# Third branch summed on VectorE, high-part products first, low parts awaited by halves, in a fused transformer kernel on one Trainium2 core

## The chip, the cores and the metric

One core of one Trainium2 chip runs the whole program. The metric is the device time of one execution in microseconds (us). The engines are called here as in the profile: PE is TensorE (matmuls), with its weight loads as PEld; DVE is VectorE, ACT is ScalarE, POOL is GpSimd, and SP only issues DMAs.

## The reference

Twelve sublayers are applied to a [256, 1024] tensor of float32: two blocks of two layers, each layer a feed-forward net, a mixing sublayer and a second feed-forward net, each between norms and with a residual. Cut to what the change touches:

```python
def swiglu_ffn(h, w_gu, w_down):
    a, b = jnp.split(h @ w_gu, 2, axis=-1)
    return (jax.nn.silu(a) * b) @ w_down

def mixing_sublayer(h, w_in, ...):            # block 1
    z = h @ w_in
    ...                                        # four branches of width 256
    gates = jax.nn.sigmoid(gz.reshape(B, S, N_BRANCH, D_MODEL))
    y = gates[:, :, 0] * (branches[0] @ w_branch[0])
    for n in range(1, N_BRANCH):
        y = y + gates[:, :, n] * (branches[n] @ w_branch[n])
    return y @ w_out
```

Block 2 is alike, with three branches and with shifts beside the norm gains.

## The kernel before

**Stages.** A stage is one sublayer; its key is block, layer, kind: `10f1`, `10m`, `10f2`, `11f1`, `11m`, `11f2`, then `20f1` to `21f2`. In the profiled execution `10m` begins at about 211 us, `10f2` at 413, `11f1` at 607, `11m` at 799, `11f2` at 1004, `20f1` at 1198, `20m` at 1392, `20f2` at 1618, `21f1` at 1808, `21m` at 1998 and `21f2` at 2223 us.

**Split numbers.** Each float32 operand is split in a high part (float32r) and a low part, the rest. A product of two operands is three matmuls that add up in PSUM: high by high, high by low, low by high (`three`). For activations the parts are `NH` and `NL`, for weights `hi` and `lo`. ACT makes `hi` from `raw` (`split_hi`), DVE makes `lo` as `raw` minus `hi` (`split_lo`, or in two halves by `split_lo_half`).

**Units.** Every stage reads 33 weight units of 128x2048 (two DMAs each, on SP's queue). A unit's `raw` and `lo` share one of five slots, `hi` has one of four. PE waits for `lo_ready` of a unit (`ready(s, u)`) before its first matmul, and releases the unit with `unit_used`.

**Where a stage begins.** The 256 tokens are two tiles t of 128. While the last matmuls of a stage run for tile 1, tile 0 is normed on DVE, transposed on PE (`turn_normed`), copied to `NH` by ACT (`normed`) and its rest put into `NL` by DVE (`normed_rest`), each in two halves of four 128-column chunks. `nh t a` and `nl t a` are the signals of tile t, half a. PE then multiplies tile 0 with units 0 to 3. Meanwhile DVE does for tile 1, in its fixed order (`entrance`): the products with the gain row (L1175), the low part of unit 2, the new X (L1193), the low part of unit 3, the mean square (L1204) that POOL turns into an inverse root, the norm (L1234; in block 2 also a shift, L1240). For stages of block 2 the new X comes before both units. PE turns tile 1 before the last quarter of unit 3 (in a mixing stage too), and then multiplies tile 1 with units 0 to 3.

**Where a mixing stage ends.** Units 25 to 28 hold the four branch projections, 29 to 32 the output projection. In block 1 PE does branches 2 and 3 together: the first half of the columns of branch 2, of branch 3, then the second halves. DVE multiplies each result, in pieces b of 128x512, with its gates (`gated`, L1688). POOL adds branches 0 and 1 (`sum 1 b`, L680) and then branch 2 (`sum 2 b`, L680 too); DVE adds branch 3 (`merged`, `y b`, L1697), ACT copies the high part (`yh b`, L1083), DVE makes the low part (`yl b`, L1700). PE starts the output projection, unit 29, when `yl 0` is there; its order is unit 29 and 30 for tile 0, 29 for tile 1, then 31 and 32 for tile 0 and the rest of tile 1.

The order on every engine is that of the code; only semaphores tie the engines. In the block-1 mixing stage the code before reads:

```python
if u == OUT1 - 1:                    # u = 28
    if s.block == 1:
        gated(G[:, 16:24, :], 2, range(0, 2))
        merged(G[:, 24:32, :], 3, "sum 2", range(0, 2))
        gated(G[:, 16:24, :], 2, range(2, 4))
```

## Time and profile before

| what | value |
|---|---|
| three timed runs | 2421.65, 2423.36, 2424.78 us, median 2423.36 |
| the profiled execution's own time | 2421.88 us |
| its span in the profile | 2420.1 us |
| mean granted TensorE clock | 0.999 |
| PE busy | 2388.7 us, 99% of the span |
| PEld busy | 2178.4 us, 90% |
| DVE busy | 1651.3 us, 68% |
| ACT busy | 1208.5 us, 50% |
| POOL busy | 233.8 us, 10% |

The span is the time from the first to the last recorded instruction. Busy times of different engines overlap. Matmuls are pipelined: a 128x512 matmul is shown with 0.39 us, but the next one starts 0.23 us after it (a 128x256 one: 0.12 us after it), so PE's rate is read from starts.

### The profile page before, as it was taken

The page shows a single profiled execution, that of the slowest core. Times are in us where ns is not written, and L with a number is a line of the kernel's source. Part 1 is how long each engine was busy: PE and PEld are TensorE (multiplying, and loading weights), DVE is VectorE, ACT ScalarE, POOL GpSimd, SP SyncE. Part 2 cuts the span into 40 slices and gives each one's busy share as a digit, 9 for nine tenths or more (in the row PEclk, how much of TensorE's full clock was granted, in tenths as well). Part 3 has the DMA queues.
Part 4 walks back from the last instruction along what each step waited for, and adds up shares of the span by engine and source line. Part 5 has one row for each costly group of instructions (what it writes and reads, how often), then busy time and mean ns, then how long its engine had stood idle before and what let it go on. Part 6 is the DMA issues. An engine that isn't in the chain of part 4 may idle for free. (4 is left out here: it accounts for less than half of the span.)

```text
span 2420.1 us, 39354 instructions
## 1 busy us (share of the span) xinstructions
PE 2388.7 (99%) x16673; PEld 2178.4 (90%) x16673; DVE 1651.3 (68%) x2158; ACT 1208.5 (50%) x1448; POOL 233.8 (10%) x334
## 2 busy tenths in 40 slices
PE   8999999999999999999999999999999999999998
PEld 6998998898899999799889899889988989988997
DVE  4786877787786697788678665575555556557554
ACT  5445565434434556444443456944444445694443
POOL 2000003000200000300110001210001000121000
PEclk9999999999999999999999999999999999999999
DMA  8895556797887564689589665456656655545653
GB/s 280 296 309 168 175 164 220 258 305 234 290 299 242 161 183 158 229 290 304 180 302 306 206 170 150 131 184 209 201 183 205 189 176 170 153 130 190 212 183 114
DMA packets 371551, 514.59 MB, mean 213 GB/s; under 512 B 23712, under 2 KB 312726, under 8 KB 371376
## 3 DMA queue, kind: packets, MB, share of 16 engines
q1 hardware_dynamic: 344976, 415.80, 53.5%
q0 software_dynamic: 26400, 96.28, 11.7%
q8 instruction: 132, 2.16, 0.4%
q14 instruction: 43, 0.35, 0.0%
HBM read 510.89 MB, written 1.13 MB: 212 GB/s over the span
## 5 line engine op out<-in xcount | busy, mean ns | idle before, releaser
L1141 DVE TENSOR_TENSOR lo<-raw,hi 128x2048 fp32r<-128x2048 f32 x382 | 876.7, 2297 | 436.4 <-ACT hi L743 435.4
L743 ACT ACTIVATE hi<-raw 128x2048 fp32r<-128x2048 f32 (+2 forms) x393 | 749.3, 1910 | 475.7 <-PE ps L1780 206.2
L1780 PE MATMUL ps<-NH,hi 128*128 128x256 f32 x3360 | 951.2, 283 | 0.0
L1780 PE MATMUL ps<-NL,hi 128*128 128x256 f32 x3360 | 942.1, 280 | 0.0
L1780 PE MATMUL ps<-NH,lo 128*128 128x256 f32 x3360 | 940.5, 280 | 0.0
L1780 PEld LDWEIGHTS ps<-NH,hi 128*128 128x128 f32 x3360 | 632.4, 188 | 13.5 <-issue 10.1
L1780 PEld LDWEIGHTS ps<-NL,hi 128*128 128x128 f32 x3360 | 633.2, 188 | 3.1
L1780 PEld LDWEIGHTS ps<-NH,lo 128*128 128x128 f32 x3360 | 634.1, 189 | 0.0
L1780 PE MATMUL ps<-hi,NH 128*128 128x512 f32 (+4 forms) x768 | 280.5, 365 | 12.4 <-DVE lo L1141 6.6
L1780 PE MATMUL ps<-hi,BH 128*128 128x512 f32 (+1 forms) x768 | 291.6, 383 | 0.0
L1780 PE MATMUL ps<-hi,BL 128*128 128x512 f32 (+1 forms) x768 | 288.6, 379 | 0.0
L1780 PE MATMUL ps<-lo,BH 128*128 128x512 f32 (+1 forms) x768 | 288.4, 379 | 0.0
L1780 PE MATMUL ps<-lo,NH 128*128 128x512 f32 (+4 forms) x768 | 274.2, 357 | 0.0
L1780 PE MATMUL ps<-hi,NL 128*128 128x512 f32 (+4 forms) x768 | 274.1, 357 | 0.0
L1294 DVE SCALAR_TENSOR_TENSOR T<-arena,T 128x512 f32<-128x512 f32 x252 | 188.5, 748 | 3.8
L1780 PEld LDWEIGHTS ps<-hi,NH 128*128 128x128 f32 x768 | 145.1, 189 | 43.4 <-DVE lo L1141 12.1
L1780 PEld LDWEIGHTS ps<-hi,BL 128*128 128x128 f32 (+1 forms) x768 | 139.3, 181 | 30.7
L805 ACT ACTIVATE BH<-arena 128x256 fp32r<-128x256 f32 x128 | 53.6, 419 | 224.8 <-DVE arena L1268 224.8
L1780 PEld LDWEIGHTS ps<-hi,NL 128*128 128x128 f32 x768 | 145.2, 189 | 22.7
L1780 PEld LDWEIGHTS ps<-lo,NH 128*128 128x128 f32 x768 | 145.4, 189 | 19.9
L1780 PEld LDWEIGHTS ps<-hi,BH 128*128 128x128 f32 (+1 forms) x768 | 139.2, 181 | 26.7 <-DVE BL L1280 0.5
L1780 PEld LDWEIGHTS ps<-lo,BH 128*128 128x128 f32 (+1 forms) x768 | 139.4, 182 | 26.3
(316 smaller groups left out, 1997.2 us busy)
## 6 DMA issues: line engine op xcount, KB each, us to landing
raw<-in_ffn_w_in SPq DMA_DIRECT2D x176, 512.0 KB, 4.9
raw<-in_ffn_w_gu SPq DMA_DIRECT2D x174, 512.0 KB, 5.7
arena<-in_ada_w POOLq DMA_DIRECT2D x72, 1024.0 KB, 6.3
raw<-in_w_in SPq DMA_DIRECT2D x92, 512.0 KB, 4.6
raw<-in_ffn_w_down SPq DMA_DIRECT2D x88, 512.0 KB, 4.4
raw<-in_ffn_w_out SPq DMA_DIRECT2D x88, 512.0 KB, 4.4
raw<-in_mix_w_in SPq DMA_DIRECT2D x86, 512.0 KB, 4.6
raw<-in_w_branch SPq DMA_DIRECT2D x16, 512.0 KB, 4.1
```

What stands on the lines that cost most here:

```text
L743: last = nc.scalar.activation(dst, src, ACT.Copy)
L805: nc.scalar.activation(BH[:, 2 * (g % 2) + j, :], HF[:, j, :], ACT.Copy).then_inc(act_done, done("act", f"bh {g} {j}"))
L1141: last = nc.vector.tensor_tensor(dst, src, part.bitcast(F32), ALU.subtract)
L1294: ins = nc.vector.scalar_tensor_tensor(out=ada_acc, in0=ADW[:, c, :], scalar=cond[:, c:c + 1], in1=ada_acc, op0=ALU.mult, op1=ALU.add)
L1780: last = nc.tensor.matmul(dst, a, b, start=start and k == 0, stop=stop and k == 2, skip_group_check=skip)
```

## The change

1. **End of the mixing stage, block 1.** POOL no longer adds branch 2. A new `third` adds it on DVE, one 128x512 addition per piece. `last_two` writes out DVE's order: products of branch 2, pieces 0 and 1, their sums, branch 3 and `y` of pieces 0 and 1, a product of branch 2, the low parts of y (`low_y`), and only then the low part of unit 30, which stood ahead of all that; then the second half of the columns. In block 2 the same work stays in the same order.
2. **High part first.** At the start of each stage, for the first chunks of unit 0 (and of unit 1 in some stages) and for both tiles, PE issues all products with `NH` first, after `nh`, and those with `NL` after them, after `nl`. The number of matmuls is the same.
3. **Halves.** The low part of unit 3 is made in two halves, as unit 1's was, and PE waits for unit 1 and unit 3 by halves (`lo half 1`, `lo half 3`). In text the title's "second and fourth unit" are units 1 and 3.
4. **Setup.** ACT copies the first half of `NH` before it waits for the second half of unit 0.

```diff
-                    if s.block == 1 and u in (BR1 + 1, BR1 + 2):
+                    if s.block == 1 and u == BR1 + 1:
...
             act.wait_ge(first_in, 32)
             nc.scalar.activation(hi[:, 0, 0:1024], raw[:, 0, 0:1024], ACT.Copy).then_inc(act_done, done("act", "hi first"))
+            normed(None, 0, range(1))
             act.wait_ge(raw_ready[0], 32)
             nc.scalar.activation(hi[:, 0, 1024:2048], raw[:, 0, 1024:2048], ACT.Copy).then_inc(hi_ready, 1)
-            normed(None, 0)
+            normed(None, 0, range(1, 2))
...
-                split_lo(s, 3)
+                for k in range(2):
+                    split_lo_half(s, 3, k)
                 mean_square_new(p, 1)
...
+            def third(pairs):
 
                 for b in pairs:
-                    gated(gates, n, (b,))
-                    mine(f"gated {n}" if b == 3 else f"gated {n} {b}")
-                    dve.wait_ge(pool_done, at("pool", f"{sum_before} {b}"))
+                    mine("gated 2" if b == 3 else f"gated 2 {b}")
+                    dve.wait_ge(pool_done, at("pool", f"sum 1 {b}"))
                     y = T8[:, 2 * b:2 * b + 2, :]
-                    nc.vector.tensor_tensor(y, y, gates[:, 2 * b:2 * b + 2, :], ALU.add).then_inc(dve_done, done("dve", f"y {b}"))
+                    nc.vector.tensor_tensor(y, y, G[:, 16 + 2 * b:18 + 2 * b, :], ALU.add).then_inc(dve_done, done("dve", f"sum 2 {b}"))
...
+            def last_two(s):
+
+                fourth = G[:, 24:32, :]
+                gated(G[:, 16:24, :], 2, range(0, 2))
+                third(range(0, 2))
+                merged(fourth, 3, None, range(0, 2))
+                gated(G[:, 16:24, :], 2, range(2, 3))
+                low_y(range(0, 2))
+                split_lo(s, OUT1 + 1)
+                gated(G[:, 16:24, :], 2, range(3, 4))
+                third(range(2, 4))
+                merged(fourth, 3, None, range(2, 4))
+                low_y(range(2, 4))
...
                 else:
                     ready(s, 0)
+                    pe.wait_ge(act_done, at("act", "nh 0 0", p))
+                    gate_up(0, 0, 0, 0, parts=range(0, 2))
                     pe.wait_ge(dve_done, at("dve", "nl 0 0", p))
-                    gate_up(0, 0, 0, 0)
-                ready(s, 1)
...
                 ready(s, 2)
                 gate_up(2, 0, 1, 0)
+                pe.wait_ge(dve_done, at("dve", "lo half 3", p))
+                gate_up(3, 1, 1, 0, range(0, 2))
                 ready(s, 3)
-                gate_up(3, 1, 1, 0, range(0, 3))
+                gate_up(3, 1, 1, 0, range(2, 3))
                 turn_normed(p, 1)
...
                 bank_free(0, 1)
+                pe.wait_ge(act_done, at("act", "nh 1 0", p))
+                gate_up(0, 0, 0, 1, parts=range(0, 2))
                 pe.wait_ge(dve_done, at("dve", "nl 1 0", p))
-                gate_up(0, 0, 0, 1).then_inc(unit_used, 1)
+                gate_up(0, 0, 0, 1, parts=range(2, 3)).then_inc(unit_used, 1)
```

**How the instructions move.** On DVE at the end of the first mixing stage (`10m`), before. `arena<-arena,ps` is a product with gates, `T8<-T8,arena` an addition, `NL<-T8,NH` a low part of y, and the first `lo<-raw,hi` is unit 30, the last three are units 31, 32 and the next stage's 0:

```order
L1141 TENSOR_TENSOR lo<-raw,hi 128x2048 [waits hi_ready]
L1688 TENSOR_TENSOR arena<-arena,ps 128x512 [waits pe_done] x3
L1697 TENSOR_TENSOR T8<-T8,arena 128x512 [waits pool_done,dve_done]
L1688 TENSOR_TENSOR arena<-arena,ps 128x512 [waits pe_done]
L1697 TENSOR_TENSOR T8<-T8,arena 128x512 [waits pool_done,dve_done]
L1700 TENSOR_TENSOR NL<-T8,NH 128x512 [waits act_done] x2
L1688 TENSOR_TENSOR arena<-arena,ps 128x512 [waits pe_done] x3
L1697 TENSOR_TENSOR T8<-T8,arena 128x512 [waits pool_done,dve_done]
L1688 TENSOR_TENSOR arena<-arena,ps 128x512 [waits pe_done]
L1697 TENSOR_TENSOR T8<-T8,arena 128x512 [waits pool_done,dve_done]
L1700 TENSOR_TENSOR NL<-T8,NH 128x512 [waits act_done] x2
L1141 TENSOR_TENSOR lo<-raw,hi 128x2048 [waits hi_ready] x3
```

And the same place after, up to the third and fourth of the additions at L1699 (the first row holds the four products of branch 1 too, which another `lo` no longer parts from those of branch 2):

```order
L1691 TENSOR_TENSOR arena<-arena,ps 128x512 [waits pe_done] x6
L1699 TENSOR_TENSOR T8<-T8,arena 128x512 [waits pool_done,dve_done] x2
L1691 TENSOR_TENSOR arena<-arena,ps 128x512 [waits pe_done]
L1732 TENSOR_TENSOR T8<-T8,arena 128x512 [waits dve_done]
L1691 TENSOR_TENSOR arena<-arena,ps 128x512 [waits pe_done]
L1732 TENSOR_TENSOR T8<-T8,arena 128x512 [waits dve_done]
L1691 TENSOR_TENSOR arena<-arena,ps 128x512 [waits pe_done]
L1705 TENSOR_TENSOR NL<-T8,NH 128x512 [waits act_done] x2
L1139 TENSOR_TENSOR lo<-raw,hi 128x2048 [waits hi_ready]
L1691 TENSOR_TENSOR arena<-arena,ps 128x512 [waits pe_done]
L1699 TENSOR_TENSOR T8<-T8,arena 128x512 [waits pool_done,dve_done] x2
```

Four additions are new on DVE (L1699), and unit 30's low part has moved behind the first two low parts of y.

On PE in stage `10f2`, from the transposes of the hidden tile (first row) to tile 1 with unit 0, before:

```order
L1840 MATMUL ps<-arena 128x128
L1780 MATMUL ps<-hi,NH 128x512 [waits dve_done]
L1780 MATMUL ps<-lo,NH 128x512
L1780 MATMUL ps<-hi,NL 128x512
L1780 MATMUL ps<-hi,NH 128x512
```

And after:

```order
L1870 MATMUL ps<-arena 128x128
L1810 MATMUL ps<-hi,NH 128x512 [waits act_done,dve_done]
L1810 MATMUL ps<-lo,NH 128x512
L1810 MATMUL ps<-hi,NH 128x512
L1810 MATMUL ps<-lo,NH 128x512
L1810 MATMUL ps<-hi,NH 128x512
L1810 MATMUL ps<-lo,NH 128x512
L1810 MATMUL ps<-hi,NH 128x512
L1810 MATMUL ps<-lo,NH 128x512
L1810 MATMUL ps<-hi,NL 128x512 [waits dve_done]
L1810 MATMUL ps<-hi,NL 128x512 x3
```

The wait for `nl 1 0` stands eight matmuls later; the `dve_done` that is left at the first one is that of the PSUM bank.

On DVE at the entry to `11f1` and its like, before and after: the low part of unit 3 between the new X and the mean square.

```order
L1193 SCALAR_TENSOR_TENSOR X<-arena,X 128x1024 [waits dve_done,pool_done]
L1141 TENSOR_TENSOR lo<-raw,hi 128x2048 [waits hi_ready]
L1204 TENSOR_SCALAR arena<-arena 128x1 [waits act_done]
L1234 SCALAR_TENSOR_TENSOR arena<-X,arena,T 128x512 [waits pre_in,pool_done]
L1234 SCALAR_TENSOR_TENSOR arena<-X,arena,T 128x512
```

```order
L1194 SCALAR_TENSOR_TENSOR X<-arena,X 128x1024 [waits dve_done,pool_done]
L1150 TENSOR_TENSOR lo<-raw,hi 128x1024 [waits hi_ready] x2
L1205 TENSOR_SCALAR arena<-arena 128x1 [waits act_done]
L1235 SCALAR_TENSOR_TENSOR arena<-X,arena,T 128x512 [waits pre_in,pool_done]
L1235 SCALAR_TENSOR_TENSOR arena<-X,arena,T 128x512
```

One instruction has become two; nothing else moved there.

## Rows read from the trace of the kernel before

**Rows 1.** The page, busy time, share of the span, instructions:

```profile
PE 2388.7 (99%) x16673; PEld 2178.4 (90%) x16673; DVE 1651.3 (68%) x2158; ACT 1208.5 (50%) x1448; POOL 233.8 (10%) x334
```

**Rows 2.** PE's waits: total us, times, longest:

```profile
PE ps L1780 <- DVE lo L1141: 6.6, 14, 0.8
PE ps L1780 <- DVE NL L1250: 2.9, 7, 1.0
```

**Rows 3.** Timeline, entry to `11f1`: start, duration, [idle before <-releaser]:

```profile
614.22 2.28 DVE L1141 TENSOR_TENSOR lo<-raw,hi 128x2048 fp32r<-128x2048 f32 x1
615.66 0.39 PE L1780 MATMUL ps<-hi,NL 128*128 128x512 f32 x1
616.56 0.50 PE L1780 MATMUL ps<-hi,NH 128*128 128x512 f32 x1 [0.51 <-DVE lo L1141]
617.23 1.42 DVE L1234 SCALAR_TENSOR_TENSOR arena<-X,arena,T 128x512 f32<-128x512 f32 x2 [0.66 <-POOL arena L510]
618.75 1.03 PE L1807 MATMUL ps<-arena 128*128 128x128 f32 x8
619.39 1.09 ACT L792 ACTIVATE NH<-ps 128x512 fp32r<-128x512 f32 x2 [3.89 <-PE ps L1807]
619.54 0.48 PE L1780 MATMUL ps<-hi,NH 128*128 128x512 f32 x1
620.33 0.38 PE L1840 MATMUL ps<-arena 128*128 128x128 f32 x2
620.86 0.47 PE L1780 MATMUL ps<-hi,NH 128*128 128x512 f32 x1
```

**Rows 4.** Timeline of DVE, a half split and the next instruction:

```profile
1196.86 1.22 DVE L1149 TENSOR_TENSOR lo<-raw,hi 128x1024 fp32r<-128x1024 f32 x1
1197.99 1.28 DVE L1250 SCALAR_TENSOR_TENSOR NL<-ps,NH 128x512 fp32r<-128x512 f32 x2
```

**Rows 5.** Timeline of PE, tile 1 turned at the entry to `20f1`:

```profile
1210.65 1.26 PE L1807 MATMUL ps<-arena 128*128 128x128 f32 x8 [0.39 <-DVE arena L1240]
1211.66 0.48 PE L1780 MATMUL ps<-hi,NH 128*128 128x512 f32 x1
...
1212.45 0.38 PE L1840 MATMUL ps<-arena 128*128 128x128 f32 x2
1212.81 0.47 PE L1780 MATMUL ps<-hi,NH 128*128 128x512 f32 x1
```

**Rows 6.** Timeline of PE, first matmul of tile 1 in `10m` and `20m`:

```profile
224.87 0.39 PE L1780 MATMUL ps<-hi,NH 128*128 128x256 f32 x1 [0.26 <-DVE NL L1250]
...
1405.85 0.39 PE L1780 MATMUL ps<-hi,NH 128*128 128x256 f32 x1 [0.35 <-DVE NL L1250]
```

**Rows 7.** Timeline, end of `10m`:

```profile
377.86 7.11 POOL L680 TENSOR_TENSOR T<-arena 128x512 f32<-128x512 f32 x4 [29.16 <-DVE arena L1688]
380.50 3.30 DVE L1141 TENSOR_TENSOR lo<-raw,hi 128x2048 fp32r<-128x2048 f32 x1 [0.93 <-ACT hi L743]
385.90 2.54 POOL L680 TENSOR_TENSOR T<-T,arena 128x512 f32<-128x512 f32 x2
391.08 0.47 PE L1780 MATMUL ps<-hi,NH 128*128 128x512 f32 x1 [0.64 <-DVE NL L1700]
395.41 0.68 DVE L1688 TENSOR_TENSOR arena<-arena,ps 128x512 f32<-128x512 f32 x1
396.12 0.69 DVE L1697 TENSOR_TENSOR T<-T,arena 128x512 f32<-128x512 f32 x1
396.73 1.47 DVE L1700 TENSOR_TENSOR NL<-T,NH 128x512 fp32r<-128x512 f32 x2
398.12 6.69 DVE L1141 TENSOR_TENSOR lo<-raw,hi 128x2048 fp32r<-128x2048 f32 x3
400.46 0.50 PE L1780 MATMUL ps<-hi,NH 128*128 128x512 f32 x1 [0.81 <-DVE lo L1141]
```

**Rows 8.** Timeline of PE, end of `11m`, units 29 and 31:

```profile
980.30 0.47 PE L1780 MATMUL ps<-hi,NH 128*128 128x512 f32 x1 [1.79 <-DVE NL L1700]
...
989.69 0.50 PE L1780 MATMUL ps<-hi,NH 128*128 128x512 f32 x1 [0.78 <-DVE lo L1141]
```

**Rows 9.** Timeline of PE, setup, units 0 and 2:

```profile
14.49 0.77 PE L1780 MATMUL ps<-hi,NH 128*128 128x512 f32 x1 [0.54 <-DVE NL L1250]
...
23.17 0.50 PE L1780 MATMUL ps<-hi,NH 128*128 128x512 f32 x1 [0.23 <-DVE lo L1141]
```

More of the change, by code:

```diff
@@ L1147, in split_lo_half @@
                 dve.wait_ge(hi_ready, n + 1)
-                part = slice(1024, 8 * VU_N if (s.kind, s.block, u) == ("m", 1, V_U) else 2048) if k else slice(0, 1024)
-                last = nc.vector.tensor_tensor(lo[:, n % LR, part], raw[:, n % LR, part], hi[:, n % HR, part].bitcast(F32), ALU.subtract)
+                (dst, src), = split_pieces(s, u, n % LR, lo)
+                (part, _), = split_pieces(s, u, n % HR, hi)
+                half = dst.shape[1] // 2
+                cols = slice(half * k, half * k + half)
+                last = nc.vector.tensor_tensor(dst[:, cols], src[:, cols], part[:, cols].bitcast(F32), ALU.subtract)
                 if k:
@@ L1152, in split_lo_half @@
                 else:
-                    last.then_inc(dve_done, done("dve", "lo half"))
+                    last.then_inc(dve_done, done("dve", f"lo half {u}"))
             def tile_out(s, t, h):
@@ L1325, in ffn @@
                     mean_square_new(p, 1)
-                    split_lo(s, 3)
+                    for k in range(2):
+                        split_lo_half(s, 3, k)
                 else:
@@ L1734, in mix @@
                         gated(G2[:, 8:16, :], 2)
-                    if u == OUT1 - 1:
-                        if s.block == 1:
-                            merged(G[:, 24:32, :], 3, "sum 2", range(2, 4))
-                        else:
-                            merged(G2[:, 16:24, :], 1, "sum 1", range(2, 4))
+                    if u == OUT1 - 1 and s.block == 2:
+                        merged(G2[:, 16:24, :], 1, "sum 1", range(2, 4))
+                        low_y(range(2, 4))
                 split_lo(s, OUT1 + 2)
@@ L1774, in ready, with three @@
                 pe.wait_ge(lo_ready, s.base + u + 1)
-            def three(dst, wh, wl, xh, xl, start, stop, weights_still=True, skip=False):
+            def three(dst, wh, wl, xh, xl, start, stop, weights_still=True, skip=False, parts=range(3)):
                 pairs = ((wh, xh), (wh, xl), (wl, xh)) if weights_still else ((xh, wh), (xh, wl), (xl, wh))
                 for k, (a, b) in enumerate(pairs):
+                    if k not in parts:
+                        continue
                     last = nc.tensor.matmul(dst, a, b, start=start and k == 0, stop=stop and k == 2, skip_group_check=skip)
@@ L1793, in channels, with tokens @@
                 return last
[L1795 removed]
+            def tokens(dst, u, n, a, w, t, chunks=range(C), parts=range(3)):
                 for c in chunks:
                     wh, wl = weights(u, n * c + a, n * c + a + w)
[L1799 removed]
+                    last = three(dst, NH[:, c, tile_of(t)], NL[:, c, tile_of(t)], wh, wl, c == 0, c == C - 1, True, skip=True, parts=parts)
                 return last
@@ L1810, in turn_normed, with gate_up @@
                     m.stage = stage
-            def gate_up(u, half, g, t, chunks=range(4)):
+            def gate_up(u, half, g, t, chunks=range(4), parts=range(3)):
                 for c in chunks:
@@ L1816, in gate_up @@
                     k = 4 * half + c
-                    last = three(ps[:, gu_bank(g, t), :], NH[:, k, tile_of(t)], NL[:, k, tile_of(t)], wh, wl, k == 0, k == C - 1, True, skip=True)
+                    last = three(ps[:, gu_bank(g, t), :], NH[:, k, tile_of(t)], NL[:, k, tile_of(t)], wh, wl, k == 0, k == C - 1, True, skip=True, parts=parts)
                 return last
```

85 lines of the change are left out of this document (55 added, 30 removed).

## The prediction

> **What bounds the kernel now.** I began with the page: PE is busy for 2388.7 of 2420.1 us [rows 1]. So the change, which takes no matmul away, can give back only time in which PE stands still, about 31 us, of which the first 10 lie before any matmul. Then came PE's waits: for low parts of weights 6.6 us in 14 waits, for low parts of activations 2.9 us in 7 [rows 2]. Where these waits lie was read from the timeline of PE: at each of the eleven stage boundaries, at the end of the two block-1 mixing stages, and in the setup; inside stages PE runs from one matmul to the next.
>
> The idle time that the view shows is less than what is lost. At the entry to 11f1 the last matmul of unit 2 starts at 615.66 and the first of unit 3 at 616.56, 0.90 us later where 0.23 is usual: 0.67 lost, 0.51 shown [rows 3]. So I add 0.16 to each idle time shown. A pair of transposes normally holds PE for 0.15 us (my estimate from their 0.38 us, which overlaps); in 11f1 the matmul after them comes 0.53 later, which is 0.38 lost without a releaser named [rows 3]: it is the wait for the low part of tile 1.
>
> What matters at every place is which wait comes next, since DVE's work for tile 1 is a chain of its own that starts from the end of the previous stage.
>
> **The change, part by part.** All is costed as PE time regained.
>
> *Entry to a block-1 feed-forward stage (10f2, 11f1, 11f2).* In 11f1 the low part of unit 3 runs from 614.22 to 616.50, and PE, ready at 615.89, starts at 616.56 [rows 3]. A half takes 1.22 us [rows 4], so the first is there at 615.44 and the second at about 616.56, when PE does not ask for it before 615.89 + 6 x 0.23 = 617.27. The 0.67 us go. What is late next is the norm of tile 1: its two halves start at 617.23 and take 1.42, the first is done at about 617.94. PE would be at the transposes at 618.75 - 0.67 = 618.08, so just behind the first half and ahead of the second. How long the transposes take then, rows of another stage show: there PE waits for both halves, and from the first transpose to the next matmul it is 1.01 us [rows 5], here now 0.79 [rows 3]. So 618.08 + 1.01 = 619.09 and some 0.05 for the later norm, against 619.54: 0.4 regained of 0.67. Then the high part first: ACT copies the first half of NH between 619.39 and about 619.94, in time, and with its wait eight matmuls later the low part is no longer waited for: 0.38. Together 0.78, three times: **2.3 us**. In 11f2 PE also waits early in the stage for tile 0's low part (the longest wait of that kind, 1.0 [rows 2]); that wait goes too, but DVE's chain there is set by weights that come late, so PE meets the chain again at unit 3; I count nothing for it.
>
> *What a half costs.* A half and the next instruction start 1.13 us apart [rows 4], full splits (6.69 - 2.28) / 2 = 2.20 apart [rows 7]: two halves cost 0.06 us more, on the chain to the norm. The Trainium skill ("VectorE: DVE Perf Modes", the section on the TRN2 errata) speaks against such a cut: it says that an operation with sources in SBUF pays a fixed extra latency per instruction, and gives (N + 151) / 0.96 ns for a float32 tensor_tensor, that is 0.16 us for each further instruction, an estimate from that page. By it the gain would be 0.7 us smaller over the seven feed-forward entries. The starts in the rows say 0.06, and these decide here.
>
> *Entry to a block-1 mixing stage (10m, 11m).* Matmuls are 256 wide there, and PE comes to the norm with more room. The stall at unit 3 (about 0.45) returns nearly whole, and the first matmul of tile 1 waits 0.26 + 0.16 [rows 6] for its low part, which ends. 0.85 twice: **1.7 us**.
>
> *Entry to a block-2 mixing stage (20m, 21m).* DVE makes the new X before both units there, so PE's stall lies at unit 2, which is not cut. Only the low part of tile 1: 0.35 + 0.16 [rows 6], and the first matmul after a stall is slower by 0.1: 0.6 twice: **1.2 us**.
>
> *Entry to a block-2 feed-forward stage (20f1, 20f2, 21f1, 21f2).* Here the norm is what PE waits for already: the transposes begin with an idle 0.39 and take 1.01 instead of 0.79 [rows 5]. The stall at unit 3 of 20f1 moves there and gains nothing; the halves cost 0.06. After the transposes of the hidden tile it is 0.36 to the next matmul [rows 5] against 0.15: 0.21 regained. 0.15 four times: **0.6 us**.
>
> *Setup.* PE starts 0.54 us earlier if it may begin on NH [rows 9], but unit 2, whose weights are still coming, holds it to 23.17 as before [rows 9]; what is left are a short wait at unit 3 and 0.38 at tile 1: **0.5 us**.
>
> *End of a block-1 mixing stage.* In 10m PE loses 0.64 + 0.16 before unit 29 and 0.81 + 0.16 before unit 31 [rows 7], together 1.8; in 11m 1.79 + 0.16 and 0.78 + 0.16 [rows 8], together 2.9. POOL's four sums of branches 0 and 1 take 7.11 us [rows 7]; two later ones take 2.54, 1.27 each [rows 7], so 5.08 of the 7.11 are their own. The low part of unit 30 falls into them and takes 3.30 instead of 2.28 [rows 7]: one waits for the other to end. With that split moved away POOL is done at 377.86 + 5.08 = 382.94. DVE has the products of branch 2 (pieces 0, 1) at about 382.2, so its first addition waits to 382.94. From there its order is a chain: two additions 1.22; for pieces 0 and 1 a product and an addition, 0.71 + 0.61 from the starts at 395.41, 396.12 and 396.73 [rows 7], 2.64; a product 0.62; two low parts 1.39 (396.73 to 398.12 [rows 7]); the low part of unit 30, 2.20; then 0.62 + 1.22 + 2.64 + 1.39. The sum is 13.9: unit 31's low part starts at 396.9 instead of 398.12 [rows 7]. The low part for unit 29 is there at about 388, before PE wants it at 390.3; unit 30's at 391, before 393.1. So the first stall goes whole and the second stays, and 398.12 - 396.87 = 1.25 is regained in 10m. In 11m DVE is earlier by its place against POOL's sums: its first addition comes while POOL's third sum runs, and POOL's fourth gets in behind it and holds the second addition for 1.27. So 1.3 there, or 2.5 if it does not get in. Together **2.55 us**, with bounds of 0 (each addition waits again) and 4.7 (both stalls of both stages).
>
> The transfers of the next stage start from two signals: unit 29 used, and the last low part of y. Both come earlier by about as much as PE, so I count nothing.
>
> **The sum.** 2.3 + 1.7 + 1.2 + 0.6 + 0.5 + 2.55 = 8.85 us. Against the profiled execution's own 2421.88 that is 2413.0; the median of the runs is 1.48 above it, and I forecast for the median: 2423.36 - 8.85 = **2414.5 us**. A measurement tells some 0.2%, 4.85 us, from no change.
>
> **Rivals.**
> 1. *The ends of the mixing stages gain nothing*: the four additions, 2.44 us more on DVE, eat what the shorter chain gives, and unit 31 is as late as before. For it: DVE is the last releaser at both stalls. Against: the waits for POOL go. Time: 8.85 - 2.55 = 6.3 gained, 2417.1. Chance 0.16.
> 2. *DVE becomes the bound and the kernel is slower.* If all four new additions had to wait for a sum of POOL, 4 x 1.27 = 5.1 us, unit 31 would come 5.1 - 1.25 = 3.9 later than now, twice 7.7, and with the norms late in the next stages most of the rest goes: about 2430. It decides once the four wait for over 1.25 together. Against: POOL has no sum left after 383, and DVE's third and fourth come at about 391. Chance 0.04.
> 3. *The stalls only move.* At each entry PE meets the norm of tile 1 instead, as in block 2 now [rows 5]: the halves give nothing, tile 1's part is hidden by later norms, and 2 to 4 us in all remain: 2420.5. For it: DVE's chain from the previous stage is fixed. Against: in 11f1 the norm is done in time for all but 0.25 us. Chance 0.12.
> 4. *All stalls go*: DVE is through with its order before PE in both mixing stages and 11f2 regains its early wait: 12 to 13 us, 2411. Chance 0.06.
>
> My own case has 0.62. The range reaches from rival 4 to the middle of rival 3: 2409.5 to 2420.5; forecast, rival 1 and rival 4 lie inside, with part of rival 3. Faster by over 4.85 us: 0.62 + 0.13 of rival 1 + 0.06, 0.81. Within: the rest of rivals 1 and 3, 0.15. Slower 0.04.
>
> **What the changed profile would show.** Right: no idle before unit 3 in block 1; no idle named after NL before tile 1 anywhere; 0.2 to 0.3 us more between the transposes and the next matmul in 11f1; unit 29 started without a wait at the end of 10m and 11m, and unit 31 still waiting for a low part, by 0.4 to 1.8; POOL's four sums in about 5.1 us instead of 7.11. Wrong: an addition of DVE after 385 that lasts over 1 us; a wait for unit 30; a new wait for NH; or ACT late with the next stage's unit 1. The forecast fails if the 0.16 that I add to each idle time, or the 0.38 at tile 1, is not PE's loss but something that stays.

## The result, and the profile after

The changed kernel takes 2412.37 us (median of 5 runs, 2410.64 to 2413.22) against 2421.96 (2421.20 to 2424.78) for the kernel before on the same chip: a ratio of 0.9957, 95% interval 0.9946 to 0.9968, or 9.6 us. The forecast was 8.85 us less, 2414.5. The profiled execution took 2412.04 us, with a span of 2410.2 us at a granted clock of 0.999.

The page's row of busy times:

```profile
PE 2385.2 (99%) x16673; PEld 2177.2 (90%) x16673; DVE 1651.8 (69%) x2178; ACT 1208.4 (50%) x1448; POOL 220.5 (9%) x326
```

and the view of PE's waits (engine, line, releaser: us in total, times, longest):

```profile
PE ps L1837 <- DVE arena L1235: 9.9, 2, 9.6
PE ps L1810 <- DVE lo L1139: 4.3, 8, 0.8
PE ps L1837 <- DVE arena L1241: 1.7, 2, 1.3
PE ps L1810 <- DVE arena L1270: 0.8, 1, 0.8
PE ps L2208 <- DVE arena L1574: 0.4, 1, 0.4
```

Beside [rows 2]: no matmul waits for NL any more, the waits for low parts of weights fell from 6.6 us in 14 to 4.3 in 8, and one of 0.8 us is new (a bias addition, L1270, in 10f1; below). The wait of 1.3 us (L1241) stands before the transposes of tile 1 in 20f1, where it was 0.39 [rows 5]: the stall of 0.53 before unit 3 there has moved to the norm, as forecast. PE is busy for 2385.2 us, 3.5 less than before; the rest of the gain is idle time.

**An entry.** PE's timeline at the entry to 11f1 (start, duration in us, engine, line, operation), which answers to [rows 3]:

```profile
615.26 0.40 PE L1810 MATMUL ps<-hi,NL 128*128 128x512 f32 x1
615.62 1.32 PE L1837 MATMUL ps<-arena 128*128 128x128 f32 x8
616.70 0.48 PE L1810 MATMUL ps<-hi,NH 128*128 128x512 f32 x1
```

There is no stall before unit 3. The transposes begin 0.13 late and hold PE for 1.08 us to the next matmul, where it was 0.79: the norm of tile 1 is what comes next, as forecast.

**An end.** The end of 10m on GpSimd, VectorE and TensorE (first the sums of branches 0 and 1; L1691 are products, L1699 the new additions, L1705 low parts of y, L1139 splits). It answers to [rows 7]:

```profile
377.50 5.06 POOL L677 TENSOR_TENSOR T<-arena 128x512 f32<-128x512 f32 x4 [29.16 <-DVE arena L1691]
...
379.85 0.69 DVE L1691 TENSOR_TENSOR arena<-arena,ps 128x512 f32<-128x512 f32 x1 [0.64 <-PE ps L1810]
381.26 0.69 DVE L1691 TENSOR_TENSOR arena<-arena,ps 128x512 f32<-128x512 f32 x1 [0.72 <-PE ps L1810]
381.87 1.84 DVE L1699 TENSOR_TENSOR T<-T,arena 128x512 f32<-128x512 f32 x2
...
388.08 2.28 DVE L1139 TENSOR_TENSOR lo<-raw,hi 128x2048 fp32r<-128x2048 f32 x1
...
394.73 1.47 DVE L1705 TENSOR_TENSOR NL<-T,NH 128x512 fp32r<-128x512 f32 x2
396.13 4.49 DVE L1139 TENSOR_TENSOR lo<-raw,hi 128x2048 fp32r<-128x2048 f32 x2
```

GpSimd's four sums take 5.06 us instead of 7.11. The low part of unit 31 starts 18.63 us after the first of them (396.13 - 377.50), where it was 398.12 - 377.86 = 20.26 [rows 7]. PE shows no wait for unit 29 and none for unit 31, so both stalls of 10m are gone.

**Where the time came from.** A span from the first transpose of one kind to the next is a clock that all these kernels share: "entry" runs from the transposes of tile 0 at the end of the stage before to those of tile 1, "rest" from there to those of tile 0 at the stage's own end. Worked out from the starts of these rows in the PE timelines, in us:

| | before | changed | changed again | ends only | entries only | no high first | order only | sum only | unit 3 whole |
|---|---|---|---|---|---|---|---|---|---|
| 10f1 rest | 181.04 | 181.77 | 180.69 | 181.86 | 180.81 | 181.06 | 180.65 | 180.69 | 180.67 |
| 10m entry | 13.53 | 12.94 | 12.95 | 13.52 | 12.91 | 12.95 | 12.94 | 12.95 | 13.51 |
| 10m rest | 190.21 | 188.17 | 188.18 | 188.76 | 190.03 | 188.76 | 190.41 | 188.12 | 188.01 |
| 10f2 entry | 13.46 | 12.91 | 12.81 | 13.45 | 13.76 | 13.76 | 12.81 | 14.30 | 14.19 |
| 11f1 entry | 13.46 | 12.80 | 12.81 | 13.45 | 12.82 | 12.80 | 12.81 | 12.82 | 13.45 |
| 11m rest | 191.11 | 188.08 | 188.89 | 189.61 | 190.83 | 188.24 | 190.71 | 187.91 | 187.74 |
| 11f2 entry | 14.62 | 14.12 | 14.41 | 14.68 | 14.71 | 14.48 | 12.81 | 14.24 | 15.00 |
| 20m rest | 213.35 | 212.81 | 212.77 | 213.35 | 212.74 | 213.28 | 212.87 | 212.90 | 212.60 |
| 20f2 entry | 13.35 | 13.42 | 13.42 | 13.35 | 13.42 | 13.41 | 13.42 | 13.43 | 13.37 |

Some rows repeat over all kernels with the same code there (10m entry and 11f1 entry to 0.04 us, 20m rest to 0.16), others differ by about 1 us and more with the same code (10f1 rest, 10f2 entry, 11m rest). That difference matters for every reading below.

A narrower window shows the ends by themselves. The same matmul is taken in the trace of before and in another trace, and the difference of its two starts is read once ahead of unit 29 and once behind the first products of unit 31 (389.13 and 403.82 us in the 10m of before, 977.42 and 990.03 in its 11m). What the difference grows by in between is what PE gained over that end, in us. The last row is how long ScalarE waited for a late transfer of w_out in 11m (3.82 in before):

| | changed | changed again | ends only | entries only | no high first | order only | sum only | unit 3 whole |
|---|---|---|---|---|---|---|---|---|
| end of 10m | 1.65 | 1.66 | 1.65 | 0.00 | 1.64 | -0.40 | 1.72 | 1.68 |
| end of 11m | 2.59 | 1.85 | 1.58 | -0.10 | 2.81 | 0.02 | 2.84 | 2.80 |
| wait for w_out, 11m | 2.90 | 3.79 | 4.06 | 3.91 | none | 3.39 | 2.68 | 2.53 |

### The profile page after: what moved, and what is told of

It is laid out like the page before. It is cut to its first block and busy times, and to the rows that moved or that the text cites. A ratio compares the mean times of both kernels' runs of the same rounds, so it can differ in the third digit from the quotient of the medians.

```text
span 2410.2 us, 39367 instructions
## 1 busy us (share of the span) xinstructions
PE 2385.2 (99%) x16673; PEld 2177.2 (90%) x16673; DVE 1651.8 (69%) x2178; ACT 1208.4 (50%) x1448; POOL 220.5 (9%) x326
## 3 DMA queue, kind: packets, MB, share of 16 engines
HBM read 510.89 MB, written 1.13 MB: 212 GB/s over the span
## 5 line engine op out<-in xcount | busy, mean ns | idle before, releaser
L1139 DVE TENSOR_TENSOR lo<-raw,hi 128x2048 fp32r<-128x2048 f32 (+1 forms) x370 | 848.4, 2294 | 435.3 <-ACT hi L740 434.1
L1810 PE MATMUL ps<-hi,NL 128*128 128x512 f32 (+4 forms) x768 | 259.3, 357 | 0.0
```

Of the source, the lines that this page charges most:

```text
L1139: last = nc.vector.tensor_tensor(dst, src, part.bitcast(F32), ALU.subtract)
L1810: last = nc.tensor.matmul(dst, a, b, start=start and k == 0, stop=stop and k == 2, skip_group_check=skip)
```

## Experiments

All times are medians beside runs of the kernel before on the same chip. There were several chips, so kernels from different ones are compared by their distance from before, which took 2422.68 us beside the first four kernels, 2422.30 beside the changed kernel run again and the three named with it, 2422.12 beside the three with transposes apart, and 2421.51 beside the kernel with the early split. The intervals of the ratios are 4 to 6.5 us wide, so a difference of 1 or 2 us between two kernels rests on the traces and not on the medians.

### The ends alone, and the entries alone

Two halves of the change. The first is the kernel before with `last_two`, `third` and GpSimd's shorter sums; the second the changed kernel with these put back:

```
                         if s.block == 1:
-                            last_two(s)
+                            gated(G[:, 16:24, :], 2, range(0, 2))
+                            merged(G[:, 24:32, :], 3, "sum 2", range(0, 2))
+                            gated(G[:, 16:24, :], 2, range(2, 4))
```

> The kernel before with only the ends of the block-1 mixing stages changed (third branch's sum on VectorE, the low part of unit 30 behind it, PE's wait for it); entries, setup and the order of products as before. Theory A (the parts are independent): the traces of before and after show PE 1.65 us earlier over the end of 10m and 2.6 over that of 11m, so 4.25 us faster than before, about 2417.7 us; POOL's first four sums take about 5.1 us, unit 29 starts without a wait, and the stalls at unit 3 and at tile 1 stay as they were. Rival B (the ends gain nothing by themselves, and what the shift showed there came from the earlier entries, which gave VectorE a lead): under 1.5 us, about 2421. Rival C (the forecast's size): 2.55 us, 2419.4.

> The changed kernel with the ends of the block-1 mixing stages put back as before (GpSimd sums branch 2, the low part of unit 30 early); setup, entries and order of products as changed. Theory A (independent parts): the pieces of the shift outside the two ends sum to about 5.4 us, so 2416.6 us, and together with the ends-only kernel the whole gain of 9.6. Rival B (the entries' gain is used up by the unchanged ends: PE arrives earlier and waits longer for units 29 and 31, since VectorE's chain there does not move): the entries of 10m and 11m give nothing, 1.7 to 2 us less, 2418.5. In the trace A has the stalls before units 29 and 31 of the length of [rows 7] and [rows 8], B has them longer by what the entry gave.

Ends only: 2419.53 us against 2422.68 (ratio 0.9988, 0.9979 to 0.9997), 3.15 less. Entries only: 2415.91 (0.9972, 0.9961 to 0.9983), 6.8 less. Together 9.9, the whole. In the kernel with entries only, the stalls of 10m and 11m are of the length of [rows 7] and [rows 8]:

```profile
389.69 0.47 PE L1788 MATMUL ps<-hi,NH 128*128 128x512 f32 x1 [0.64 <-DVE NL L1706]
399.08 0.50 PE L1788 MATMUL ps<-hi,NH 128*128 128x512 f32 x1 [0.81 <-DVE lo L1142]
...
977.79 0.47 PE L1788 MATMUL ps<-hi,NH 128*128 128x512 f32 x1 [1.89 <-DVE NL L1706]
987.18 0.50 PE L1788 MATMUL ps<-hi,NH 128*128 128x512 f32 x1 [0.78 <-DVE lo L1142]
```

So the parts add up (theory A of both), and rival B of both falls. The size in theory A of the first, 4.25, was read from one pair of traces and is too high: in the ends-only kernel the ends are worth 1.65 in 10m and 1.58 in 11m, 3.2, which is what its median shows, where 2.55 was forecast. (Its 10m rest is shorter by 1.45 only, because PE loses 0.2 more there between 248 and 258 us, far from the end; the entries-only kernel has the same loss.)

### High part first, and the halves of unit 3

```
-                pe.wait_ge(act_done, at("act", "nh 1 0", p))
-                gate_up(0, 0, 0, 1, parts=range(0, 2))
                 pe.wait_ge(dve_done, at("dve", "nl 1 0", p))
-                gate_up(0, 0, 0, 1, parts=range(2, 3)).then_inc(unit_used, 1)
+                gate_up(0, 0, 0, 1).then_inc(unit_used, 1)
```

and so at tile 0 and in the mixing stages:

> The changed kernel with the products of the first chunks in their old order (low parts of the activations waited for before the first product), in every entry but the setup; the halves of units 1 and 3 and the ends stay. Theory A (high part first is worth the idle at tile 1, and halves the rest): 0.38 in three block-1 feed-forward entries, 0.42 in two mixing entries, 0.6 in two of block 2 and 0.21 in four, together 4.0 us over the changed kernel, 2416.4. Rival B (the halves alone let the norm come early enough, so the low part of tile 1 is there in time too): within 1 us of the changed kernel, 2412.4 to 2413.4.

2417.66 us (0.9979, 0.9970 to 0.9988), 5.0 under before, where the changed kernel is 9.6 to 9.7 under: 4.6 over the changed kernel. Theory A said 4.0, and the 0.6 between them is within the noise; rival B falls. The waits for NL are back, in the view of waits and in two rows of PE's timeline, one of 10f2's tile 0 and one of 20m's tile 1:

```profile
PE ps L1810 <- DVE NL L1251: 3.1, 5, 1.5
```

```profile
414.44 0.47 PE L1810 MATMUL ps<-hi,NH 128*128 128x512 f32 x1 [0.76 <-DVE NL L1251]
1403.36 0.39 PE L1810 MATMUL ps<-hi,NH 128*128 128x256 f32 x1 [0.35 <-DVE NL L1251]
```

In the mixing stages it costs 0.4 in 10m (its rest is 0.59 longer, of which 0.2 is the loss between 248 and 258 us named above) and 0.47 to 0.51 in 20m. In 10f2 and 11f2 PE now also waits 0.76 and 1.5 for the low part of tile 0, which the sum left out; but these entries, 13.76 and 14.48 us, are no longer than in some kernels with the high part first (up to 14.30 and 14.71), so that these waits cost time is not shown. The runs of this kernel lie between 2414.45 and 2419.51, and the profiled one also waits 1.9 for a bias addition in 11f1.

The halves of unit 3 undone, and in the mixing stages PE's wait for unit 1 by halves too; the rest kept:

```
-                for k in range(2):
-                    split_lo_half(s, 3, k)
+                split_lo(s, 3)
...
-                pe.wait_ge(dve_done, at("dve", "lo half 3", p))
-                gate_up(3, 1, 1, 0, range(0, 2))
                 ready(s, 3)
-                gate_up(3, 1, 1, 0, range(2, 3))
+                gate_up(3, 1, 1, 0, range(0, 3))
```

> The changed kernel with unit 3's low part whole again and waited for whole (and in the mixing stages unit 1 waited for whole too); high part first and the ends stay. Theory A (my sum): 0.4 more in three block-1 feed-forward entries and 0.43 in two mixing ones, less 0.06 for each half saved in 9 places: 2.1 - 0.5 = 1.5 us over the changed kernel, 2413.9. Rival B (the stall only moves to the norm of tile 1, so that the halves give nothing): within 0.4 us, 2412.4 to 2412.8. Rival C (the whole stall of 0.67 comes back in each of five): 3.3 us over, 2415.7. In the trace A has a wait for a low part at unit 3 in block 1 and transposes of 11f1 without a wait.

2414.99 us (0.9967, 0.9955 to 0.9979). Its profiled execution took 7173.94 us where its other five took 2413.55 to 2416.62, and nothing is read from it; the kernel was run once more.

> The same kernel as the one without halves of unit 3, whose profiled execution was of no use (7174 us). Theory A as there: 0.4 us more in each of three block-1 feed-forward entries and two mixing entries, 0.06 less in nine; read from the stretches between the transposes of tile 0 and tile 1: 10f2 and 11f1 13.2 to 13.3 (changed 12.91 and 12.80, before 13.46 twice), 10m and 11m 13.4 (changed 12.95, before 13.52), block 2 as before within 0.1. Rival B (only moved to the norm): the stretches up to the transposes as before, but the next ones shorter by as much, with no difference to the changed kernel over both.

2414.91 us (0.9969, 0.9958 to 0.9981): 2.3 over the changed kernel run beside it, and by the distance from before 1.9 the first time; theory A said 1.5, rival C 3.3. The stall is back before unit 3, here in 11f1, and the entries of 10m and 11f1 are as long as before (13.51 and 13.45):

```profile
614.61 0.50 PE L1808 MATMUL ps<-hi,NH 128*128 128x512 f32 x1 [0.51 <-DVE lo L1139]
```

In 11f1 and 10m the halves are worth 0.65 and 0.56 at the entry, and the rest of the stage gives back about 0.15 in 10m. The rival by which the stall only moves falls for block 1. It holds for block 2: there the entry to 20f2 is 13.42 with halves and 13.37 without, so the halves gain nothing and cost 0.05 to 0.07 us a pair, the 0.06 of the forecast. By the Trainium skill ("VectorE: DVE Perf Modes", the section on the TRN2 errata) it would be about 0.16, an estimate from its formula; the stages here show a third of it.

### What of the ends does it: the order, or the sum

Once with the third branch summed on GpSimd again (cut to two lines here) and the low part of unit 30 in its new place; once with the sum on VectorE and unit 30's low part in its old place:

```
-                third(range(0, 2))
-                merged(fourth, 3, None, range(0, 2))
+                merged(fourth, 3, "sum 2", range(0, 2))
```

```
                 low_y(range(0, 2))
-                split_lo(s, OUT1 + 1)
...
-                        if u < OUT1 - (2 if s.block == 1 else 1):
+                        if u < OUT1 - 1:
                             split_lo(s, u + 3)
```

> The changed kernel with the third branch summed on GpSimd again, as before; the low part of unit 30 stays behind the first half of the y pieces, and all else stays. Theory A (the gain of the ends comes from taking unit 30's split out of GpSimd's four sums): GpSimd's sums take 5.1 us, its sums of branch 2 end 2.5 later and hold VectorE's first y pieces, VectorE has 2.4 us less work of its own; unit 31's low part starts 18.8 us after GpSimd's first sum in 10m (changed 18.6, before 20.3): within 0.5 us of the changed kernel over both stages. Rival B (the gain comes from not waiting for GpSimd's sum of branch 2): unit 31's low part starts at 20 us or later, and 1.5 to 3 us of time come back.

> The changed kernel with the low part of unit 30 in its old place, ahead of the products of branch 2; the third branch stays summed on VectorE, and all else stays. Theory A (the order carries the gain): GpSimd's four sums take 7.1 us again and the split 3.1 to 3.3; unit 29 waits 0.5 us in 10m and 0.9 in 11m, unit 31's low part starts 18.9 us after GpSimd's first sum; 0.5 to 1.5 us slower than the changed kernel. Rival B (the sum on VectorE carries it): within 0.3 us of the changed kernel. Rival C (additions of VectorE now lie against GpSimd's late sums as well, and each pair costs another 1.27): over 2.5 us slower.

Order only: 2415.05 us (0.9970, 0.9958 to 0.9981), 2.4 over the changed kernel run beside it. Over the end of 10m it loses 0.40 us against before, over that of 11m it is even (0.02). 11f2's entry, which follows the longer stall, takes 12.81 instead of 14.41 and gives part of it back; that the one comes of the other is likely but not shown. Sum only: 2413.58 us (0.9964, 0.9951 to 0.9976), with 1.72 and 2.84 gained over the two ends, as much as in the changed kernel. Its median is 1.0 over the changed kernel's, inside what theory A said (0.5 to 1.5) and outside rival B's 0.3, so the time does not decide between them. The traces do: in the profiled execution what is lost lies elsewhere, in 10f2's entry (14.30) and in 11f1 (180.53 for its rest against 178.51), with weights that landed late in both, and PE waits for neither unit 29 nor unit 31, where theory A had waits of 0.5 and 0.9. Theory A, my own, falls in both, and the mechanism of rival B holds in both. The order-only kernel in 10m:

```profile
376.64 5.05 POOL L680 TENSOR_TENSOR T<-arena 128x512 f32<-128x512 f32 x4 [29.16 <-DVE arena L1694]
382.62 2.54 POOL L680 TENSOR_TENSOR T<-T,arena 128x512 f32<-128x512 f32 x2
387.73 1.67 POOL L680 TENSOR_TENSOR T<-T,arena 128x512 f32<-128x512 f32 x1 [2.56 <-DVE arena L1694]
...
384.03 1.70 DVE L1733 TENSOR_TENSOR T<-T,arena 128x512 f32<-128x512 f32 x1 [1.54 <-POOL T L680]
...
397.30 2.28 DVE L1142 TENSOR_TENSOR lo<-raw,hi 128x2048 fp32r<-128x2048 f32 x1
...
399.64 0.50 PE L1811 MATMUL ps<-hi,NH 128*128 128x512 f32 x1 [1.61 <-DVE lo L1142]
```

GpSimd's first four sums take 5.05 us, as the new order promised, but VectorE gains nothing by it: it waits 1.54 for GpSimd's sum of branch 2, its first addition then takes 1.70 instead of 0.69, and the pair of low parts of y takes 2.39 instead of 1.28 beside the next sum. Unit 31's low part starts 20.66 us after GpSimd's first sum, and PE waits 1.61 in one piece for what it waited 0.64 and 0.81 before. The sum-only kernel:

```profile
376.18 7.11 POOL L677 TENSOR_TENSOR T<-arena 128x512 f32<-128x512 f32 x4 [29.16 <-DVE arena L1691]
...
378.82 3.30 DVE L1139 TENSOR_TENSOR lo<-raw,hi 128x2048 fp32r<-128x2048 f32 x1 [0.93 <-ACT hi L740]
382.05 1.27 DVE L1691 TENSOR_TENSOR arena<-arena,ps 128x512 f32<-128x512 f32 x2
383.24 1.28 DVE L1699 TENSOR_TENSOR T<-T,arena 128x512 f32<-128x512 f32 x2
...
394.74 4.49 DVE L1139 TENSOR_TENSOR lo<-raw,hi 128x2048 fp32r<-128x2048 f32 x2
```

The split and the four sums do hold each other up (3.30 and 7.11), and it costs nothing: VectorE would stand idle there for the branch products (0.64 and 0.72 in the changed kernel), and when it has its two products the sums are done. Unit 31's low part starts 18.56 us after GpSimd's first sum. What held VectorE was GpSimd's sum of branch 2, as VectorE's additions of branch 3 in the kernel before show, one for each half of the columns:

```profile
387.31 1.70 DVE L1697 TENSOR_TENSOR T<-T,arena 128x512 f32<-128x512 f32 x1 [1.71 <-POOL T L680]
...
393.79 1.70 DVE L1697 TENSOR_TENSOR T<-T,arena 128x512 f32<-128x512 f32 x1 [0.28 <-POOL T L680]
```

It idles 1.99 us for the sums, and each of the two additions then takes 1.70 instead of 0.69 beside GpSimd's next sum, 2.02 more. Of these 4.0 us the four new additions cost 2.4 (0.61 from one start to the next), and 1.6 are left: what unit 31's low part gained (20.26 - 18.63), and PE with it (1.65). So half of what moving the sum removes is the wait, and half is contention with that sum. The Trainium skill ("SBUF — State Buffer", the section "SBUF: two separate sides") says that VectorE, in an operation with two inputs in SBUF, and GpSimd take a shared port for a whole instruction, and the other waits. The trace agrees: the products, which read PSUM, keep their 0.69 us beside GpSimd's sums, and the additions do not.

### The changed kernel once more

> The changed kernel once more, unaltered, for the spread of its stages. Theory A: what the trace of the changed kernel lost inside 10f1 (1.1 us, with a wait of PE of 0.83 at 67.6 for a bias addition behind a late weight transfer) and what it gained over 11m (3.03 us) hang on when DMA lands weights, so they differ here: 10f1 between its two tile-1 and tile-0 transposes takes 181.0 to 181.9, 11m 188.1 if ScalarE gets the weights of unit 29 without a long wait (under 3 us after its last one) and 189.6 if with one of about 4. Rival B: both are fixed by the program; 181.77 and 188.08 again within 0.1. The entries repeat within 0.1 us by both. Time by both 2411 to 2415.

2412.62 us (0.9965, 0.9952 to 0.9979). From 10m on the entries, and 10m itself, repeat within 0.1 us, but for 11f2's entry (14.12, then 14.41). 10f1 and 11m do not: theory A. In 10f1 ScalarE got a unit's weights late in the first trace, and PE waited for a bias addition of VectorE that is queued behind that unit's low part (first both rows of the changed kernel, then ScalarE's of this run):

```profile
62.90 1.92 ACT L740 ACTIVATE hi<-raw 128x2048 fp32r<-128x2048 f32 x1 [10.57 <-DMA raw<-in_ffn_w_gu]
...
67.62 0.36 PE L1810 MATMUL ps<-NH,hi 128*128 128x256 f32 x1 [0.83 <-DVE arena L1270]
```

```profile
60.33 1.91 ACT L740 ACTIVATE hi<-raw 128x2048 fp32r<-128x2048 f32 x1 [8.15 <-DMA raw<-in_ffn_w_gu]
```

That was 1.1 us (181.77 against 180.69). In 11m it was the other way round. This run, with the wait for w_out on ScalarE, GpSimd's sums, VectorE's additions and PE at unit 31:

```profile
956.28 1.91 ACT L740 ACTIVATE hi<-raw 128x2048 fp32r<-128x2048 f32 x1 [3.79 <-DMA raw<-in_w_out]
...
961.19 5.51 POOL L677 TENSOR_TENSOR T<-arena 128x512 f32<-128x512 f32 x4 [30.14 <-DVE arena L1691]
...
964.44 2.82 DVE L1699 TENSOR_TENSOR T<-T,arena 128x512 f32<-128x512 f32 x2
...
982.00 0.51 PE L1810 MATMUL ps<-hi,NH 128*128 128x512 f32 x1 [0.79 <-DVE lo L1139]
```

and the first run of the changed kernel:

```profile
956.94 1.92 ACT L740 ACTIVATE hi<-raw 128x2048 fp32r<-128x2048 f32 x1 [2.90 <-DMA raw<-in_w_out]
...
961.86 5.05 POOL L677 TENSOR_TENSOR T<-arena 128x512 f32<-128x512 f32 x4 [29.25 <-DVE arena L1691]
...
965.99 2.07 DVE L1699 TENSOR_TENSOR T<-T,arena 128x512 f32<-128x512 f32 x2
```

Unit 31's low part starts 18.62 us after GpSimd's first sum there and 18.47 here, nearly the same; but with the late weights VectorE splits unit 29 late, its products and so GpSimd's first sum come 0.9 us later against PE (961.19, where the first matmul of the branch product is at 960.69; in the first run 961.86 and 962.24), and PE waits 0.79 for unit 31. The kernel before was profiled with late weights too (a wait of 3.82 us on ScalarE), as were ends only (4.06) and entries only (3.91). So of the 3.03 us between the two traces in 11m, 0.8 goes with when a transfer landed: over the end alone the gain is 1.58 and 1.85 in the two kernels with these ends and a wait of 3.79 us or more, and 2.59 to 2.84 in the four where it was 2.90 or less.

### What is left at the entries

The transposes of tile 1 set apart, with the last products of unit 3 between them:

```
-                turn_normed(p, 1)
+                turn_normed(p, 1, range(0, 1))
                 gate_up(3, 1, 1, 0, range(3, 4)).then_inc(pe_done, done("pe", "gu 1"))
+                turn_normed(p, 1, range(1, 2))
```

> The changed kernel with the two groups of transposes of tile 1 at each entry set apart: first half, the last products of unit 3, then the second half; nothing else. Theory A (what holds PE at these transposes is the second half of the norm): the stretch from the first transpose to the next matmul, 1.01 us in block 2 and 1.07 in the block-1 feed-forward entries against 0.79 where no one waits, gives 0.22 back in four entries, 0.28 in three and 0.15 in two: 2.0 us faster than the changed kernel, about 2410.6. Rival B (the second half of NH then comes so late that PE waits for it at tile 1, and the stall only moves): within 0.5 us.

2412.84 us (0.9958, 0.9946 to 0.9971): the same as the changed kernel within the noise; the 2.0 us forecast do not come. The trace, laid against both of the changed kernel, shows why, and that each theory has its place. In six of the seven feed-forward entries PE is ahead by another 0.15 to 0.23 us behind the transposes and stays so: theory A. In the four mixing entries it is ahead by up to 0.29 and then falls back by 0.26 to 0.35 at the second half of tile 1's chunks (in 21m two matmuls start 0.28 and 0.23 us before the next one where 0.12 is usual): as in rival B, though the profile names no wait at these gaps, so that their cause is not shown. About 0.4 us is gained in all.

In addition unit 2 in halves behind a block-2 stage, and the shifted norm half by half:

```
-                    split_lo(s, 2)
+                    for k in range(2):
+                        split_lo_half(s, 2, k)
...
+                    if shifted:
+                        mine(f"scaled {t} {a}")
+                        nc.vector.tensor_tensor(HN[:, t, part], HN[:, t, part], row_shift[:, part], ALU.add)...
```

> The kernel with the transposes apart, and unit 2's low part in halves at the five entries behind a block-2 stage, and the norm of a block-2 stage made half by half (scale and shift of the first half before those of the second). Theory A: PE's wait for the low part of unit 2, 0.42 to 0.48 five times, goes, and the transposes do not wait in its place, since the norm's first half is done 0.6 us earlier: 2.1 us over the kernel with the transposes apart, some 4.1 faster than the changed kernel, 2408.5. Rival B (as in block 2 so far, the norm is what PE waits for; the 0.45 appears before the transposes): no more than the kernel with the transposes apart, 2410.6.

2410.58 us (0.9951, 0.9938 to 0.9963), 2.3 under the kernel with the transposes apart on the same chip, where theory A said 2.1 for this step, and some 2 us under the changed kernel, half of the 4.1 that it said for both. The waits for unit 2's low part are gone; the entries to 20f2 and 21f2 are 12.95 and 12.95 us against 13.42, and the end of 11f2 is 0.8 shorter.

With `split_lo(s, OUT1 + 1)` back in its old place, by the same two edits as in the sum-only kernel:

> The fastest version so far (transposes of tile 1 apart, halves of unit 2, the block-2 norm half by half) with the low part of unit 30 back in its old place inside GpSimd's four sums. Theory A (that split fills time in which VectorE would idle for the branch products, and its place gives nothing): GpSimd's sums take 7.1 instead of 5.1 us, unit 31's low part starts 18.6 us after the first of them as with the split behind, PE waits neither for unit 29 nor for unit 31 in 10m; within 0.7 us of 2410.6. Rival B (the place does matter when the weights of unit 29 land late in 11m, since the split is then added to the late chain): a wait of PE for unit 29 in 11m, as the 0.68 in the kernel with all transposes apart, and 0.5 to 1 us slower.

2410.28 us (2408.91 to 2410.39; 0.9951, 0.9937 to 0.9964), 11.2 under before where the version without the early split is 11.5 under: no difference. Unit 31's low part starts 18.56 us after GpSimd's first sum, and PE waits for neither unit 29 nor unit 31: theory A. Rival B, which needs late weights in 11m, was not put to the test here (ScalarE waited 3.17 us for them). Where they were late with the early split, in the next kernel (3.74), PE did wait 0.68 for unit 29, and with the late split it did not (3.79 and 4.06 us), though it waited for unit 31 then.

That next kernel has the same early split and sets the transposes of tile 0 apart as well ("the one before" in its expectation is the kernel with unit 2 in halves):

```
-                turn_normed(s.key, 0)
+                turn_normed(s.key, 0, range(0, 1))
                 out_part(o + 3, 1, range(2, 4)).then_inc(unit_used, 1)
+                turn_normed(s.key, 0, range(1, 2))
```

> As the one before, with the transposes of tile 0 at each stage's end apart too, and the low part of unit 30 in its old place. Theory A: at the ends of 11f2, 20f1, 20f2 and 21f1 PE loses 0.22 in the transposes and 0.24 to 0.6 ahead of them (0.85, 0.47, 0.50 and 0.47 from the last matmul, where 0.24 is usual); 2.2 us more, about 6.3 faster than the changed kernel, 2406.3. Rival B (the second half of NH for tile 0 comes too late for the next stage's unit 0 or 1): the same as the one before or slower. The place of unit 30's split gives nothing by both.

2417.55 us (0.9980, 0.9971 to 0.9989), 4.6 under before, so 6.7 us slower than the same kernel with these transposes together: rival B. VectorE and ScalarE at the entry to 11f1 (L1251 makes NL, L789 NH, half by half):

```profile
605.61 0.69 DVE L1251 SCALAR_TENSOR_TENSOR NL<-ps,NH 128x512 fp32r<-128x512 f32 x1
607.43 0.69 DVE L1251 SCALAR_TENSOR_TENSOR NL<-ps,NH 128x512 fp32r<-128x512 f32 x1 [1.13 <-ACT NH L789]
...
606.80 0.60 ACT L789 ACTIVATE NH<-ps 128x512 fp32r<-128x512 f32 x1 [1.22 <-PE ps L1837]
```

PE itself no longer waits at these transposes (0.49 to 0.73 us at four stages' ends without the change), but ScalarE and VectorE run their lists in order: VectorE stands 1.13 us before NL's second half, with the low parts of units 1, 2 and 3 and the norm of tile 1 behind it, and the entries to 10m, 11f1 and 11m grow from 12.9 to 13.9 us, those to 20f2 and 21f2 from 12.95 to 14.17; those to 20m and 21m do not grow.

## Why the prediction was right, step by step

The time measured, 2412.4, is 2.1 us under the forecast and inside its range. Of these, 1.4 is the kernel before, which took 2421.96 beside it and not the 2423.36 that I started from; the gain itself was 9.6 for 8.85. The parts are these (between the profiled executions, the shift of the same matmul from one trace to the other).

- *Block-1 feed-forward entries*: 0.67, 0.77 and 0.6 where 0.78 each was said. The norm came next, the transposes took 0.29 longer (0.2 to 0.3 was said), tile 1's wait went.
- *Mixing entries*: 0.97 and 0.98 for 0.85 in block 1; 0.54 and 0.57 for 0.6 in block 2.
- *Block-2 feed-forward entries*: 0.13, 0.14, 0.15 and 0.17 for 0.15. *Setup*: 0.49 for 0.5, with units 1 and 2 still waited for (0.55 and 0.81).
- *Ends of 10m and 11m*: this is the term that was mis-sized: 2.55 said, 3.2 measured by the ends alone; the two traces show 4.25 (1.65 and 2.6), of which 0.74 goes with a transfer that landed in time and 0.27 with a longer wait for unit 31 in the ends-only kernel (1.06 us where the changed kernel run again has 0.79). Unit 31's low part starts 1.63 us earlier against GpSimd, not 1.25, so that in 10m it is in time for PE and the stall that I kept there (0.4 at least) is gone. Two steps of my chain were too long by 0.2 each: the first addition, which I let start only when GpSimd's last sum ends, starts before and ends 0.55 behind it, and the first pair of low parts takes 1.20 and not 1.39. The 11m step said 1.3, or 2.5 if GpSimd's fourth sum does not get in behind VectorE's first addition. Both occur: the first two additions, 1.28 us where nothing disturbs them, take 2.82 where the weights are late and 2.07 where they are not.
- *The reason given for the ends* was wrong in part. I followed the chain rightly, but put the gain down to the split of unit 30 leaving GpSimd's sums; by itself that gives nothing. The gain is the sum of branch 2, for which VectorE no longer waits and with which its additions no longer collide. I had both in one sum and never costed one without the other, and that the size came out as near as it did is partly luck.
- *Nothing was said of 10f1 and 20f1*. 10f1 lost 1.1 by a late transfer in that one execution. 20f1 gained 0.7 in its body; it does so in the ends-only kernel too (178.73 us against 179.39), whose code there is that of before, so it is not the change. Why the profiled execution of before was slow there stays open.

Rival 1 (the ends give nothing) and rival 2 fall with the ends-only kernel. Rival 3 (stalls only move) is refuted in block 1 and true in block 2, as the forecast had it. Rival 4 (all stalls go, 2411) was nearer than its chance of 0.06: PE waits for neither unit 29 nor unit 31 in the first trace, in 10m in the second too; its other half, the early wait of 11f2, did not come back (its entry is 14.12 and 14.41 us for 14.62).

## What to carry to other kernels

When a change moves an operation off one engine and reorders another, cost each of the two alone: here the sum was near and the credit went to the wrong half. An engine that idles for a third one can take contention for nothing, so ask what the collision delays, not how long it lasts. And an instruction that is free to come later on its own engine is not free if engines with ordered lists wait for it: the second half of the transposes of tile 0, 1.4 us later on PE in block 1, cost 1.0 to 1.2 us at five of the eleven entries.

## What the runs showed that was not expected

Kernels with the same code in a stretch differ there by up to 1.5 us (10f2's entry from 12.81 us to 14.30, with ScalarE waiting 1.91 us for weights ahead of the longest and not at all ahead of the 12.81 of the changed kernel run again), while others repeat to 0.04 us. One profiled pair can so credit a change with 0.8 us of luck in one stage and charge it 1.1 in another. One execution in about 150 took 7173.94 us, three times the usual, at a granted clock of 1.000; the next ones of the same kernel were ordinary, and its cause was not looked into.
